# Two transformer blocks in one kernel: 512-column matmuls for the upper weight part, with both activation parts side by side

## What is computed

```
def swiglu_2(h, w_gate, w_up, w_down):           # d_ff = 2816
    return (jax.nn.silu(h @ w_gate) * (h @ w_up)) @ w_down

x = x + even_mixer(...)    # ends in  concat([o_a, o_b]) @ w_out
x = x + swiglu_2(rmsnorm(x, ffn_norm[layer]), ...)
x = x + mla_mixer(...)     # ends in  attention @ w_o
x = x + swiglu_2(rmsnorm(x, ffn_norm[layer]), ...)
```

## Time and profile before

| | us |
|---|---|
| median of 3 runs | 1036.9 (1036.25 to 1043.39) |
| the profiled execution's own time | 1039.4 |
| its span (first to last instruction) | 1037.6 |
| PE busy / DVE busy / ACT busy | 949.3 / 678.7 / 512.6 |
| mean granted TensorE clock | 0.96 of full |

### The profile page before, as it was taken

One profiled execution on the slowest core, in us unless ns is written; L12 is line 12 of the kernel. 1 busy time (PEld: TensorE's weight loads), 2 busy tenths in 40 slices (PEclk: granted clock), 3 DMA queues, 4 the chain that ended last, 5 costly groups with the idle time before them and its releaser, 6 DMA issues. The chain is left out here.

```text
span 1037.6 us, 20336 instructions
## 1 busy us (share of the span) xinstructions
PE 949.3 (91%) x7615; PEld 925.7 (89%) x7615; DVE 678.7 (65%) x1323; ACT 512.6 (49%) x952; POOL 59.6 (6%) x53
## 2 busy tenths in 40 slices
PE   6798887999999979857999999999879999999997
PEld 5698887999999979755999999999768899999997
DVE  4399755666756557567656766556898657667552
ACT  4643254445444436566635544445376635445443
POOL 0017500000000010000000000000100000000000
PEclk9899988999999989879999999999889999999999
DMA  7243341676666637400457665665330346765661
GB/s 207 79 125 87 117 114 51 176 210 184 183 186 182 193 92 214 140 1 1 132 144 202 191 194 168 181 191 153 108 118 2 84 144 196 205 176 168 185 190 53
DMA packets 275319, 148.56 MB, mean 143 GB/s; under 512 B 5961, under 2 KB 273210, under 8 KB 275258
## 3 DMA queue, kind: packets, MB, share of 16 engines
q1 hardware_dynamic: 274330, 146.02, 48.7%
q0 software_dynamic: 608, 1.52, 0.5%
q10 hardware_dynamic: 320, 0.20, 0.1%
HBM read 146.39 MB, written 1.06 MB: 142 GB/s over the span
## 5 line engine op out<-in xcount | busy, mean ns | idle before, releaser
L461 PE MATMUL bank<-x0h,whi 128*128 128x256 f32 (+1 forms) x1080 | 311.4, 288 | 20.3 <-DVE wlo L1448 10.6
L462 PE MATMUL bank<-x0l,whi 128*128 128x256 f32 (+1 forms) x1080 | 309.1, 286 | 0.0
L463 PE MATMUL bank<-x0h,wlo 128*128 128x256 f32 (+1 forms) x1080 | 308.8, 286 | 0.0
L1448 DVE TENSOR_TENSOR wlo<-raw,whi 128x1024 fp32r<-128x1024 f32 (+3 forms) x184 | 204.4, 1122 | 99.1 <-ACT whi L1062 98.8
L461 PEld LDWEIGHTS bank<-x0h,whi 128*128 128x128 f32 x1080 | 208.6, 193 | 24.5 <-issue 15.7
L1062 ACT CAST whi<-raw 128x1024 fp32r<-128x1024 f32 (+3 forms) x184 | 174.6, 961 | 81.2 <-PE bank L463 78.2
L463 PEld LDWEIGHTS bank<-x0h,wlo 128*128 128x128 f32 x1080 | 208.7, 193 | 0.0
L462 PEld LDWEIGHTS bank<-x0l,whi 128*128 128x128 f32 x1080 | 207.6, 192 | 0.0
L1584 DVE TENSOR_TENSOR wlo<-raw,whi 128x1024 fp32r<-128x1024 f32 x108 | 132.0, 1222 | 65.3 <-ACT whi L1144 64.5
L461 PE MATMUL bank<-x1h,whi 128*128 128x256 f32 x532 | 156.8, 295 | 17.2 <-DVE un L2051 4.5
L463 PE MATMUL bank<-x1h,wlo 128*128 128x256 f32 x532 | 154.4, 290 | 0.0
(11 more groups left out here) (247 smaller groups left out, 1283.0 us busy)
## 6 DMA issues: line engine op xcount, KB each, us to landing
raw<-in_ffn_w_gate SPq DMA_DIRECT2D x44, 512.0 KB, 4.2
raw<-in_ffn_w_up SPq DMA_DIRECT2D x44, 512.0 KB, 4.6
raw<-in_ffn_w_down SPq DMA_DIRECT2D x32, 448.0 KB, 4.2
raw<-in_w_gate SPq DMA_DIRECT2D x22, 512.0 KB, 3.9
raw<-in_w_up SPq DMA_DIRECT2D x22, 512.0 KB, 4.1
raw<-in_w_in SPq DMA_DIRECT2D x20, 512.0 KB, 3.9
raw<-in_even_w_in SPq DMA_DIRECT2D x18, 512.0 KB, 4.1
raw<-in_ffn_w_down SPq DMA_DIRECT2D x16, 512.0 KB, 4.5
```

The lines of the kernel that those rows point to most:

```text
L461: pe.matmul(o, w[0], x[0], start=first, stop=False, skip_group_check=True)
L462: pe.matmul(o, w[0], x[1], start=False, stop=False, skip_group_check=True)
L463: return pe.matmul(o, w[1], x[0], start=False, stop=last, skip_group_check=True)
L1448: ins = v.tensor_tensor(l_, x, h_.bitcast(F32), ALU.subtract)
```

## The change

The upper and lower activation parts of a step k are put side by side in one tensor (`x0`, `x1`, `ar`; for 256 tokens 512 adjacent columns per k). In the stages named in `WIDE` (gu0, gu1, gu2, eout, down1, down2, mo) `mm2` takes the place of `mm3`: one matmul of 512 columns, w_hi with [x_hi | x_lo], which fills a whole bank, and one of 256 columns, w_lo with x_hi, into the bank's first half. The two halves of the bank must then be added. In the gu stages ACT copies the second half to SBUF (`half`) and DVE adds it to the first (`added`); the factor is multiplied in afterwards from SBUF (`scaled`), and the bank is free once `halves_added` counts. In eout, down1, mo and down2 DVE adds first one half and then the other to the residual. down0 and all other stages keep `mm3`.

```
+        x0f = sb("x0", [P, 2 * KT * TM], F32R)
+        x1f = sb("x1", [P, 2 * KT * T], F32R)
+        xi = x0f[:, :].rearrange("p (k a t) -> p k a t", a=2, t=TM)
+        x0, x1 = (w_[:, 0:2 * KT * T].rearrange("p (k a t) -> p k a t", a=2, t=T) for w_ in (x0f, x1f))
+        arf = sb("ar", [P, 2 * HW_], F32R)
+        hid = arf[:, :].rearrange("p (k a t) -> p k a t", a=2, t=T)
...
+        WIDE = ("gu0", "gu1", "gu2", "eout", "down1", "down2", "mo")
...
+            def mm2(o, w, x, first, last):
+                if not first:
+                    pe.matmul(o[:, 0:T], w[1], x[:, 0], start=False, stop=False, skip_group_check=True)
+                ins = pe.matmul(o[:, 0:2 * T], w[0], x, start=first, stop=last, skip_group_check=True)
+                if first:
+                    ins = pe.matmul(o[:, 0:T], w[1], x[:, 0], start=False, stop=False, skip_group_check=True)
+                return ins
...
             def gu_body(f, i, x, j0=0):
-                        pe.wait_ge(g("g1_done" if j % 2 == 0 else "u1_done"), FT * f + 2 * i + j // 2 - 1)
+                        pe.wait_ge(g("halves_added"), 4 * i + (2 * FT * f + j - 3))
...
             (ACT, swiglu_steps)
+                def half(i, j):
+                    act.wait_ge(prod, 4 * i + (e0 + j + 1))
+                    act.copy(tmp[j], halves(TILE0[f"gu{f}"] + j)[1]).then_inc(g("half_copied"), 1)
                 def body(i):
                     loop_hi(i, 3)
+                    half(i, 0)
                     loop_hi(i, 4)
                     if isinstance(i, int) and i == 0:
                         factor(n, rB[:, 0:T])
+                    half(i, 1)
+                    loop_hi(i, 5)
                     silu(i, 0)
-                    loop_hi(i, 5)
+                    half(i, 2)
+                    loop_hi(i, 6)
                     hidden(i, 0)
+                    half(i, 3)
                     silu(i, 1)
-                    loop_hi(i, 6)
                     hidden(i, 1)
...
             (DVE, phase_product)
-                v.tensor_tensor(res[:, m, :], res[:, m, :], acc_bank(ph, m), ALU.add).then_inc(g("res_done"), 1)
+                a_, b_ = halves(TILE0[PHASE[ph]] + m)
+                v.tensor_tensor(res[:, m, :], res[:, m, :], a_, ALU.add).then_inc(own, 1)
+                n = tick()
                 if m:
                     join(ph, m - 1)
+                v.wait_ge(own, n)
+                v.tensor_tensor(res[:, m, :], res[:, m, :], b_, ALU.add).then_inc(g("res_done"), 1)
...
             (DVE, swiglu_steps)
+                    v.wait_ge(g("half_copied"), 4 * i + (2 * FT * f + j + 1))
+                    v.tensor_tensor((g1, u1)[j % 2][kk], bank[(t0 + j) % 4][:, 0:T], tmp[j], ALU.add).then_inc(g("halves_added"), 1)
+                def scaled(i, j):
+                    v.wait_ge(g("halves_added"), 4 * i + (2 * FT * f + j + 1))
+                    v.tensor_tensor((g1, u1)[j % 2][kk], (g1, u1)[j % 2][kk], rB[:, 0:T],
                                     ALU.mult).then_inc(g("g1_done") if j % 2 == 0 else g("u1_done"), 1)
```

More of the change, by code:

```diff
@@ L192, in build @@
         MQ, MK, MQR, MKR = 0, 8 * T, 16 * T, 20 * T
-        x0hf, x0lf = (w_[:, :, :].rearrange("p k t -> p (k t)") for w_ in (x0h, x0l))
-        x1hf, x1lf = (w_[:, :, :].rearrange("p k t -> p (k t)") for w_ in (x1h, x1l))
         va_ = [un[:, TM * j:TM * (j + 1)] for j in range(8)]
@@ L414, in acc_bank, with halves @@
             return acc_tile(PHASE[ph], m)
+        def halves(t):
+            return bank[t % 4][:, 0:T], bank[t % 4][:, T:2 * T]
         def qk_offset(n):
@@ L489, in kt_outer @@
                     for j in range(nt):
-                        ins = mm3(acc(t + j, n), wt((s + j) % R, k * P),
-                                  (x[0][:, k, c0:c0 + n], x[1][:, k, c0:c0 + n]), k == 0, k == KT - 1)
+                        if stage in WIDE:
+                            ins = mm2(acc(t + j, 2 * T), wt((s + j) % R, k * P), x[:, k], k == 0, k == KT - 1)
+                        else:
+                            ins = mm3(acc(t + j, n), wt((s + j) % R, k * P),
+                                      (x[:, k, 0, c0:c0 + n], x[:, k, 1, c0:c0 + n]), k == 0, k == KT - 1)
                         if k == KT - 1:
@@ L505, in square_sum, with tile8 @@
                 return add
-            def tile8(s, r, t, x, n=T, c0=0):
+            def tile8(s, r, t, x, n=T, c0=0, wide=False):
                 pe.wait_ge(lo_done, s + 1)
                 for k in range(KT):
-                    ins = mm3(acc(t, n), wt(r, k * P), (x[0][:, k, c0:c0 + n], x[1][:, k, c0:c0 + n]),
-                              k == 0, k == KT - 1)
+                    if wide:
+                        ins = mm2(acc(t, 2 * T), wt(r, k * P), x[:, k], k == 0, k == KT - 1)
+                    else:
+                        ins = mm3(acc(t, n), wt(r, k * P), (x[:, k, 0, c0:c0 + n], x[:, k, 1, c0:c0 + n]),
+                                  k == 0, k == KT - 1)
                 ins.then_inc(prod, 1)
@@ L586, in taps @@
                 ins.then_inc(g("taps_done"), 1)
-            kt_outer("in", (x0h, x0l), lambda k: pe.wait_ge(g("xt_lo"), k + 1), TM, 0,
+            kt_outer("in", xi, lambda k: pe.wait_ge(g("xt_lo"), k + 1), TM, 0,
                      (g("res_copied"), 4))
@@ L604, in _ @@
                 if j >= 16:
-                    tile8(j, j % R, j, (x0h, x0l), T, META)
+                    tile8(j, j % R, j, xi, T, META)
                 else:
-                    tile8(j, j % R, j, (x0h, x0l), TM, 0)
+                    tile8(j, j % R, j, xi, TM, 0)
                 if j in (6, 10, 14, 18):
@@ L700, in body @@
                         if first:
[L702 removed]
+                            pe.wait_ge(g("halves_added"), 2 * FT * (f + 1) - 3 + m)
                         else:
@@ L724, in _ @@
             stat_rows(0)
-            gate_up(0, (x0h, x0l), x_ready(0), (g("sq_done"), SQ0["y0"] + 8), 1)
+            gate_up(0, x0, x_ready(0), (g("sq_done"), SQ0["y0"] + 8), 1)
             down_stage(0)
@@ L728, in _ @@
             stat_rows(2)
-            X = (x0h, x0l)
+            X = x0
             kt_outer("ein", X, x_ready(1), bank_free=(g("sq_done"), SQ0["y1"] + 8), nt=3, after=square_sum("x1"))
@@ L1178, in x_hi @@
                 act.wait_ge(g("x_turned"), k + 1)
-                act.activation(x0h[:, k, :], bank[k][:, 0:TM], ACT.Copy, scale=col("pre_mix_norm", k)).then_inc(g("xt_hi"), 1)
+                act.activation(xi[:, k, 0], bank[k][:, 0:TM], ACT.Copy, scale=col("pre_mix_norm", k)).then_inc(g("xt_hi"), 1)
             act.wait_ge(g("gain_copied"), 1)
@@ L1652, in x_lo @@
                 v.wait_ge(g("xt_hi"), k + 1)
-                v.scalar_tensor_tensor(x0l[:, k, :], bank[k][:, 0:TM], col("pre_mix_norm", k),
-                                       x0h[:, k, :].bitcast(F32), ALU.mult, ALU.subtract).then_inc(g("xt_lo"), 1)
+                v.scalar_tensor_tensor(xi[:, k, 1], bank[k][:, 0:TM], col("pre_mix_norm", k),
+                                       xi[:, k, 0].bitcast(F32), ALU.mult, ALU.subtract).then_inc(g("xt_lo"), 1)
             def x_keep(k):
```

66 lines of the change are left out of this document (33 added, 33 removed).

## The result

The changed kernel took 1030.2 us at the median (1026.4 to 1035.6 over 17 runs); the kernel before, run beside it on the same chips, 1042.5 us (1036.3 to 1044.7, 17 runs). The ratio is 0.990, with an interval from 0.988 to 0.992: 1.0% faster, between 8.4 and 12.1 us. The forecast was a gain of 16.9 us. So the direction was right and the size was about 1.6 times too large.

What follows compares the result with a forecast made beforehand. TensorE's matmul pace was taken as the bound in the touched stages; -10.3 (x1, hidden) - 6.6 (x0) + 0.7 - 1.5 + 0.8 = -16.9 us took the median 1036.9 to 1020.0, range 1004 to 1041, likeliest case 1012 to 1028.

Steps and rivals of the forecast that it cites:

- TensorE's pace is the time in the touched stages: In all seven changed stages TensorE's pace sets the time, apart from a few waits at a gu stage's start.
- The wide step, 213.3 + 13.3 = 226.6 ns: 512-column matmul in the seven changed stages: columns alone 213.3 ns plus a fixed extra of 13.3 per matmul.
- if the narrow matmul's own step rises when its neighbour is wide: Stated condition for a wrong forecast: the 256-column matmul, taken at 120.0 ns, gets slower beside a 512-column one.
- the small terms (+0.7 - 1.5 + 0.8): In us: x0 matmuls that stay three 0.7 more, three gu stage starts 1.5 less, wait behind down2 0.8 more.
- x0 in its new place takes 120.0 ns where three narrow ones stay: In ein and mdown, 456 matmuls go from 118.4 to 120.0 ns: 0.7 us more.
- DVE and ACT in a body are hidden: Gu body of four tiles: added adds and copies make DVE's chain 9.7 us, under TensorE's 11.1, 1.4 to spare.
- A gu stage's start, 0.5 us each: Wait before tile 4 goes as the add frees the bank: 1.5 us less over three stages, bounds 0 and 3.
- The tail, 0.8 us more: Behind down2 nothing covers the later residual of the last tile: wait before the last small sum grows 0.8 us.
- The base time: Starting point of the forecast: profiled execution 1039.4 us, median 1036.9; minus 16.9 gives 1020.0.
- Rival 1: Extra is a price per column: 512 columns cost 240.0 ns, time 1040.6 us, or 1036.2 if x0 keeps its step; chance 0.26.
- Rival 2: Extra vanishes in the 512-column matmul: step 213.3 ns, another 20.4 us saved, time 999.6 us; chance 0.12.
- rival 3: DVE chain bounds gu loops: body 12.1 us against 11.4, time 1054; over 1% loss from 0.75 us per body; chance 0.10.

Runs made afterwards that it cites:

- The reordering: Changed kernel with the first gu body's adds, splits and factor copy reordered, next body's first slot cast and split early: 1025.4 us, ratio 0.986 to the kernel before.
- the block of 512 columns: Kernel of matmuls alone on constant data, 64 fp32r matmuls of 512 columns in a row, new weight block each: step 226.7 ns.

## Why the prediction was right or wrong

**TensorE's pace is the time in the touched stages: right.** All body lengths are 32 pairs times the step, in every variant but the one without the narrow matmul. Where the clock is full in both, the stage differences follow from the steps within 0.3 us, but for gu1, gu2 with their starts.

**The wide step, 213.3 + 13.3 = 226.6 ns: right alone, wrong beside a narrow one. This is the step that failed.** Measured 226.7 in a block of its own, 226 in the kernel without the narrow matmuls, and 233.8 (x) or 236.0 (hidden) in the changed kernel. The prediction added two steps that were measured, or bounded, each in a row of its own kind; it did name "if the narrow matmul's own step rises when its neighbour is wide" as what would make it wrong. It was the other one that rose; the narrow one even fell from 120.0 to 116.2 or 117.2. The sum by the measured pairs:

- x0, 768 pairs: 355.2 - 350.0 = 5.2 ns, 4.0 us less (forecast 6.6)
- x1, 416 pairs (gu2 and eout): 360.0 - 350.0, 4.2 us less (forecast 13.4 x 416 = 5.6)
- hidden, 352 pairs: 360.0 - 353.2 = 6.8 ns, 2.4 us less (forecast 13.4 x 352 = 4.7)

That is 10.6 us where the forecast had 16.9, 6.3 of the missing 6.7 us. Why the wide one takes 7 to 9 ns more in that company is not shown; operands, output half and order each move it in some places and not in others. With the small terms (+0.7 - 1.5 + 0.8) the sum stays 10.6 us, and 10.2 was measured (8.4 to 12.1).

**x0 in its new place takes 120.0 ns where three narrow ones stay: right.** The end of mdown in the changed kernel:

```profile
726.90 0.28 PE L466 MATMUL bank<-x,wlo 128*128 128x256 f32 x1
...
727.26 0.28 PE L466 MATMUL bank<-x,wlo 128*128 128x256 f32 x1
```

0.36/3 = 120 ns.

**DVE and ACT in a body are hidden: right, with some luck in the size.** The chain is 10.4 us long, not 9.7, so 0.8 us a body were to spare and not 1.4. The working counted DVE's instructions at 0.33 us and two waits for ACT. It left out that an instruction which needs the result of the one ahead starts later (in the changed kernel 0.45 to 0.52 us there), and it gave no reason for dropping the third wait of the earlier trace rows, 1.82 us in each body. That wait did vanish with the new order. Had it stayed, 10.61 us and 1.3 us of adds would have been 11.9, an estimate from these rows, and more than TensorE's 11.19.

**A gu stage's start, 0.5 us each: right.** The wait before tile 4 is gone, that before tile 7 is left with 1.07 us (0.54 in the earlier trace rows), and the rest of tile 5 shows as 0.4 us. Net of the loop's gain gu1 starts 0.6 and gu2 0.5 us earlier. That the wait before tile 7 doubled was not foreseen: TensorE now comes to it sooner. The reordering then showed that 1.7 us a stage were to be had.

**The tail, 0.8 us more: right in size.** The wait before the last small sum was 1.82 us:

```profile
1023.55 1.01 PE L543 MATMUL bank<-onec,ssq 128*128 128x1 f32 x4 [2.48 <-DVE ssq L1494]
```

2.48 where 2.6 was forecast; start to start from the last product it is 0.77 us more.

**The base time.** The forecast was made from a profiled execution of 1039.4 and a median of 1036.9 from three runs. Over 17 runs before stood at 1042.5. So 1036.9 was at the low end of what one kernel shows, and the point forecast of 1020.0 is 5.5 us lower than the same sum on the later median (1025.6). The prediction also said that it would be wrong if the clock fell where it was full. In the profiled execution it did, at the start of gu0 and of ein: 95.0 against 82.3 us at half clock in all, worth up to 6.3 us, which with the 6.3 us of the pair is about the 12.3 by which the profiled execution missed the forecast 1022.5.

**The rivals.** Rival 1, a price per column, is refuted by the block of 512 columns (226.7, not 240), although its time of 1040.6 is no farther from the measured 1030.2 than the forecast's 1020.0: the pair of 353 in down2 is half way from 346.6 to 360. Rival 2 is refuted by the same block, and rival 3 by the run without copies and adds. Rival 3's threshold for a loss over 1% was also miscounted: 10.4 us and the 6 won elsewhere, over 33 bodies, are 0.5 us a body above the old one, not 0.75. No chance hung on it.

## What to carry to other kernels

When an instruction is to be merged, measure the new one in the company it will have: steps measured in rows of equal instructions need not add up (here the wide one rose by 7 to 9 ns, the narrow one fell by 3 to 4), and the company took back almost 40% of the gain. Before reading a difference of 1% from few runs, list how long each execution ran at half clock, at which places, and compare stages where both ran at full clock. If work is added to a side engine on the strength of its spare time, take the bounding engine's work away in one run to see how long the chain really is, or look where the side engine catches up after a stage's start: there it runs at its own pace, before any change is made.

## What the runs showed of the hardware

- Fp32r matmuls with a new weight block each have a fixed extra of 13.3 ns over their columns at full clock from 256 to 512 columns (but 11.9 at 272 and 20.0 at 448). Bf16 ones have 2.5. At 128 and 192 columns the step is 111.6 ns, so something per matmul, not the stream, sets it.
- The place of the operand changes it: 256 columns shifted by 16 took 113.3 ns, with a stride of 272 117.5, instead of 120.0. A block of only 32 or 64 weight columns also took 113.3 with 256 columns; 32 weight columns with 512 took 231.7, more than the 226.7 of the full block.
- Matmuls of 512 columns step in 226.7 ns among themselves, but in 232 to 236 in a kernel where narrow ones alternate with them, and in 230 even in runs of eight.
- A sequence of narrow and wide matmuls has two paces, 346.7 and 353.3 ns a pair. The same operands had the quick one behind two short matmuls and the slow one in nine other places.
- At one and the same place the same program spent 6.8 us at 1.2 GHz in one execution and 17.0 in another. The stage took 4.8 us longer, 0.5% of the kernel's time.
